# A one-layer hybrid recurrent step: the RWKV head norm reordered, delta-net inputs loaded at another place, state waits narrowed

## The reference, cut to what matters

```python
# end of RWKV (C), per head of 64 columns
mu  = mean(o_c);  var = mean(square(o_c - mu))
o_c = (o_c - mu) * rsqrt(var + GN_EPS) * ln_w + ln_b
bonus = sum(r_c * k_c * r_k) * v_c
y_c = (o_c + bonus) * g_c                      # g_c = sigmoid(g_low) @ rwkv_g_up
# start of gated DeltaNet (A): causal convolution of width 4, then SiLU
full = concatenate([conv_buf, qkv]);  new_conv = full[:, t:]
# A and B: the samples start from a given state and return the new one
# merge of the three branches
m = sum_i sigmoid(P_gate_i) * (y_i @ w_branch[i]);  h = h + m @ w_out
```

## Time and profile before

| | us |
|---|---|
| median of three runs (lowest, highest) | 3218.73 (3212.09, 3221.67) |
| the profiled execution's own time | 3215.23 |
| span of the profiled execution | 3213.4 |
| PE busy in the span | 3080.0 |
| DVE, ACT, POOL busy | 1671.0, 1182.4, 109.9 |

### The profile page before, as it was taken

The page is one execution under the profiler, slowest core; times in us unless marked ns, Lnnn a source line. Parts: engine busy times, 40 slices in busy tenths (PEclk is TensorE's granted clock), DMA queues, the critical chain, the costliest instruction groups (busy, mean ns, idle before and its releaser), DMA issues.

```text
span 3213.4 us, 61472 instructions
## 1 busy us (share of the span) xinstructions
PE 3080.0 (96%) x24976; PEld 2966.6 (92%) x24976; DVE 1671.0 (52%) x2174; ACT 1182.4 (37%) x1589; POOL 109.9 (3%) x176
## 2 busy tenths in 40 slices
PE   8999999999899999999889998997999999999998
PEld 7999999999899888888888988886999999999998
DVE  5455445454545665555575546456455444445543
ACT  4343333333434532222253224344343333333333
POOL 1000000001000000000000001011000000000001
PEclk9999999999999999998989989989999999999999
DMA  5555555655455533334553336357545655555553
GB/s 166 166 157 169 172 157 164 171 161 171 124 170 149 152 109 95 90 105 117 166 148 95 101 115 184 108 175 252 165 131 161 170 165 170 158 169 157 167 170 112
DMA packets 599915, 482.51 MB, mean 150 GB/s; under 512 B 29010, under 2 KB 545597, under 8 KB 599389
## 3 DMA queue, kind: packets, MB, share of 16 engines
q1 hardware_dynamic: 575760, 428.45, 45.7%
q0 software_dynamic: 8592, 33.16, 3.4%
q10 hardware_dynamic: 15392, 18.43, 1.6%
HBM read 451.82 MB, written 28.10 MB: 149 GB/s over the span
## 4 chain that ended last, share of the span: by engine, by line
PE 85%; DVE 7%; ACT 3%; issue 2%; DMA 2%; ACTq 0%; POOL 0%; DVEq 0%; POOLq 0%
PE ps L392 25%; PE ps L393 24%; PE ps L394 24%; PE ps L1111 2%; DVE lo L749 2%; ACT hi L559 1%; PE ps L1106 1%; PE ps L1392 0%; DMA smA<-in_dt_bias 0%; PE ps L551 0%; PE ps L2308 0%; PE ps L1405 0%; DMA rawsD<-kept 0%; PE ps L1935 0%; DVE raws L773 0%
## 5 line engine op out<-in xcount | busy, mean ns | idle before, releaser
L392 PE MATMUL ps<-xh,hi 128*128 128x288 f32 x4800 | 1456.4, 303 | 45.7 <-ACT kept L630 11.2
L393 PE MATMUL ps<-xl,hi 128*128 128x288 f32 x4800 | 1430.0, 298 | 0.0
L394 PE MATMUL ps<-xh,lo 128*128 128x288 f32 x4800 | 1429.1, 298 | 0.0
L749 DVE TENSOR_TENSOR lo<-raw,hi 128x1024 fp32r<-128x1024 f32 (+1 forms) x820 | 975.1, 1213 | 542.8 <-ACT hi L559 533.2
L559 ACT ACTIVATE hi<-raw 128x1024 fp32r<-128x1024 f32 (+1 forms) x820 | 832.5, 1042 | 843.3 <-PE ps L394 797.6
L392 PEld LDWEIGHTS ps<-xh,hi 128*128 128x128 f32 x4800 | 915.9, 191 | 77.8 <-issue 25.1
L393 PEld LDWEIGHTS ps<-xl,hi 128*128 128x128 f32 x4800 | 916.2, 191 | 0.6
L394 PEld LDWEIGHTS ps<-xh,lo 128*128 128x128 f32 x4800 | 915.8, 191 | 0.0
L393 PE MATMUL ps<-hidl,hi 128*128 128x288 f32 x1376 | 406.9, 296 | 0.0
L392 PE MATMUL ps<-hidh,hi 128*128 128x288 f32 x1376 | 406.9, 296 | 0.0
L394 PE MATMUL ps<-hidh,lo 128*128 128x288 f32 x1376 | 404.3, 294 | 0.0
(11 more groups left out here) (680 smaller groups left out, 2022.0 us busy)
## 6 DMA issues: line engine op xcount, KB each, us to landing
raw<-in_w_ff_up SPq DMA_DIRECT2D x688, 256.0 KB, 4.1
raw<-in_w_in SPq DMA_DIRECT2D x448, 256.0 KB, 3.0
raw<-in_w_ff_down SPq DMA_DIRECT2D x344, 256.0 KB, 3.4
raw<-in_w_out SPq DMA_DIRECT2D x64, 256.0 KB, 3.0
raw<-in_w_branch SPq DMA_DIRECT2D x48, 256.0 KB, 3.0
gatesD<-kept ACTq DMA_DIRECT2D x24, 288.0 KB, 3.0
gates<-gatesD POOLq DMA_DIRECT2D x8, 864.0 KB, 7.2
raw<-in_w_branch SPq DMA_DIRECT2D x48, 128.0 KB, 3.4
```

The lines of the kernel that those rows point to most:

```text
L392: pe.matmul(out, w, rh, start=start, stop=False)
L393: pe.matmul(out, w, rl, start=False, stop=False)
L394: return pe.matmul(out, wl, rh, start=False, stop=stop)
L749: dve.tensor_tensor(lo[:, q, 0:wide], raw[:, q, 0:wide], hi[:, q, 0:wide].bitcast(F32), SUB).then_inc(lo_ready[q], 1)
```

## The change

The tail of RWKV takes another order: the product r·k·r_k is made before the mean, in a tile of its own (`rsF`); its head sum and the multiplication by v go ahead of the root; weight with bonus, and bias with gate, become one operation each, on six slices. PE no longer waits for `C_recurred`. The unit counts there become 2, 5, 2, 3 and 8. POOL loads `rowsA` and `smA` when RWKV's tail begins, A's projections when its last sum is made, and the first two sample states of A at `mixer_done`. The 36 tile copies of the delta-net head become two; the copy of the last rows moves behind the second turn of the loop, and an empty SiLU stands ahead of the loop. The wait for the prompt's state in A moves down to the first write that needs it, and in B it goes; B's first sample state is loaded without it. The units behind each pair of sample states in B rise from 4 to 8 (`bsso`). In `branch` ACT makes the merged high part after the next split; `out` loses its wait at the start. The waits on `sums_read` and `hn_sum` are counted anew.

```diff
@@ pe_program, phase
-                if not (down or name.startswith("up") and name != "up00" and name != "up10"):
+                if not (down or name == "out" or name.startswith("up") and name != "up00" and name != "up10"):
                     pe.wait_ge(acc_empty, p["group0"])
@@ act_program
+            def merged_high(k):
+                act.wait_ge(sem("gated"), k + 1)
+                pair = slice(2 * k, 2 * k + 2)
+                act.activation(xh[:, pair, :], merged[:, pair, :], ACT.Copy).then_inc(sem("merged_hi"), 1)
...
                             split(ahead(p, s, it))
                         if name == "branch":
+                            if s % 2 == 0 and it * 4 + s // 2:
+                                merged_high(it * 4 + s // 2 - 1)
...
-                        if name == "branch":
-                            act.wait_ge(sem("gated"), it * 4 + (g + 1))
-                            pair = bass.ds((it * 4 + g) * 2, 2)
-                            act.activation(xh[:, pair, :], merged[:, pair, :], ACT.Copy).then_inc(sem("merged_hi"), 1)
+                        if name == "branch" and it * 4 + g == KD // 2 - 1:
+                            merged_high(it * 4 + g)
@@ U
-  rec=6, fin=4, fin2=15, bsso=4
+  rec=2, fin=5, fin2=2, fin3=3, fin4=8, bsso=8
@@ pe_mixC
             weave(U["rec"])
-            e.need("C_recurred")
...
             weave(U["fin"])
-            e.need("hn_sq")
+            e.need("hn_sq", 2)
...
             weave(U["fin2"])
-            e.need("hn_sq")
+            e.need("sums_read", 2)
             for p in range(BT):
-                mm = pe.matmul(ps[:, p, 0:NT], ones64[:, :], sqF[:, p, :], start=True, stop=True)
+                mm = pe.matmul(ps[:, p, 0:NT], ones64[:, :], rsF[:, p, :], start=True, stop=True)
...
@@ dve_mixC
+            for p in range(BT):
+                ins = dve.scalar_tensor_tensor(rsF[:, p, :], proj[:, p, 0:NT], par1[:, R_RK + p:R_RK + p + 1], proj[:, 6 + p, 0:NT], MUL, MUL)
...
+            weave(U["rec"])
+            e.need("hn_sum", 2)
+            e.link(dve.scalar_tensor_tensor(Y, PS6, -1.0 / 64, Y, MUL, ADD))
+            e.mark(dve.tensor_tensor(sqF[:, :, :], Y, Y, MUL), "hn_sq")
+            dve.wait_ge(sem("C_so8_stored"), 6)
+            dve.nop().then_inc(sem("C_recurred"), 1)
             weave(U["fin"])
+            weave.presplit(2)
             e.need("hn_sum", 2)
-            e.mark(dve.tensor_tensor(sqF[:, :, :], PS6, proj[:, 12:18, 0:NT], MUL), "gn_bonus_used")
-            e.link(dve.tensor_tensor(Y, Y, sqF[:, :, :], ADD))
+            e.mark(dve.tensor_tensor(rsF[:, :, :], PS6, proj[:, 12:18, 0:NT], MUL), "gn_bonus_used")
+            weave(U["fin2"])
+            e.need("fin_rs")
+            e.link(dve.tensor_tensor(Y, Y, sqF[:, :, :], MUL))
+            for p in range(BT):
+                e.link(dve.scalar_tensor_tensor(Y[:, p, :], Y[:, p, :], par1[:, R_LNW + p:R_LNW + p + 1], rsF[:, p, :], MUL, ADD))
+            weave(U["fin3"])
             e.need("hn_sum")
-            e.link(dve.tensor_tensor(Y, PS6, Y, MUL))
+            for p in range(BT):
+                e.link(dve.scalar_tensor_tensor(Y[:, p, :], Y[:, p, :], par1[:, R_LNB + p:R_LNB + p + 1], ps[:, p, 0:NT], ADD, MUL))
+            weave(U["fin4"])
             dve.nop().then_inc(sem("mixer_done"), 1)
@@ pool_A
-            pool.wait_ge(sem("mixer_done"), 1)
             pool.dma_start(rowsA[0:24, :], ...).then_inc(sem("a_landed"), 16)
+            for k, name in ((0, "a_log"), (1, "dt_bias")):
+                pool.dma_start(smA[:, k, :], i[name][0].partition_broadcast(P)).then_inc(sem("a_landed"), 16)
             pool.wait_ge(sem("kept_stored"), 16 * GROUPS_A)
+            e.need("hn_sum", 5)
             for k in range(4):
                 pool.dma_start(proj[:, 6 * k:6 * k + 6, :], projA[:, 6 * k:6 * k + 6, :]).then_inc(sem("projA_landed"), 16)
...
+            pool.wait_ge(sem("mixer_done"), 1)
+            load_state(pool, tA[1], 0, "A", state_in, 3)
+            load_state(pool, tA[1], 1, "A", state_in, 3)
             e.need("rows_kept")
@@ pe_mixA
             pe.wait_ge(sem("a_landed"), 48)
+            pe.wait_ge(sem("mixer_done"), 1)
@@ act_mixA
             e.link(act.activation(smA[:, 0, :], smA[:, 0, :], ACT.Exp))
-            e.need("last_turned")
-            e.mark(act.activation(rowsA[0:27, :], psf[0:27, 512:512 + 2304], ACT.Copy), "rows_kept")
+            e.link(act.activation(spare, ones[:, 0:1], ACT.Silu))
+            e.need("last_kept", 2)
...
+                if m == 1:
+                    e.need("last_turned")
+                    e.mark(act.activation(rowsA[0:27, :], psf[0:27, 512:512 + 2304], ACT.Copy), "rows_kept")
                 weave(U["conv"])
@@ dve_mixA: two copies for 36; b == 2
+            e.link(dve.tensor_copy(tails[:, :, :, 0:GAP], ps[:, 0, 0:432].rearrange("p (m b t) -> p m b t", b=NSEQ, t=GAP)))
+            e.mark(dve.tensor_copy(lastA[:, :, GAP:27].rearrange("p m (b t) -> p m b t", t=GAP), tails[:, :, :, TS:]), "last_kept")
...
                     dve.nop().then_inc(sem("state_whole"), 1)
-                    dve.wait_ge(sem("state_stored"), 1)
...
+                if b == 2:
+                    dve.wait_ge(sem("state_stored"), 1)
                 e.link(dve.tensor_tensor(t["kb"][0:n, :, :], region(2, n, P), bc(R("nb"), 2, P), MUL))
@@ pool_B
+            load_state(pool, tB[1], 0, "B", state_in, 2)
             pool.wait_ge(sem("out_stored"), 16 * stored)
-            pool.nop().then_inc(sem("state_stored"), 2)
+            load_state(pool, tB[1], 1, "B", state_in, 2)
@@ dve_mixB
             rest_y(dve, 0, BT)
+            weave.presplit(2)
             e.need("B_gl")
...
                     dve.nop().then_inc(sem("state_whole"), 1)
-                    dve.wait_ge(sem("state_stored"), 2)
```

More of the change, by code:

```diff
@@ L1212, in dve_solve @@
             weave(next(units))
-        U = dict(feat=6, hist=12, shift=60, rec=6, root=3, bfeat=8, lora=6, lora2=3, kk=8, prod=7, tok=2,
-                 wz=2, z=1, scz=1, sco=2, s0t=2, ssz=2, szt=2, sso=3, s8t=2, fin=4,
+        U = dict(feat=6, hist=12, shift=60, rec=2, root=3, bfeat=8, lora=6, lora2=3, kk=8, prod=7, tok=2,
+                 wz=2, z=1, scz=1, sco=2, s0t=2, ssz=2, szt=2, sso=3, s8t=2, fin=5,
                  conv=3, head=8, hl=8, aba=4, gc=6, aprod=7, az=4, ascz=2, asco=6, assz=2, asso=3,
-                 bgk=20, fin2=15, hn=8, afin=6, afin2=8, bfin=2, bfin2=16, bprod=4, bsco=6, bsso=4)
+                 bgk=20, fin2=2, fin3=3, fin4=8, hn=8, afin=6, afin2=8, bfin=2, bfin2=16, bprod=4, bsco=6, bsso=8)
         def pool_mixers(pool):
@@ L1519, in act_mixC @@
             act_root_of(e, act, sqF, 1.0 / 64, 1, 2, weave)
-            weave(U["fin2"] - U["root"] + 2 * U["fin"])
+            weave(U["fin2"] + U["fin3"] + U["fin4"] - U["root"])
         def act_root_of(e, act, sq_, scale, k, sums, weave):
@@ L1734, in dve_mixC @@
                     e.mark(ins, "hn_sq")
+            weave(U["rec"])
[4 more added lines that the diff above has]
+            dve.nop().then_inc(sem("C_recurred"), 1)
             weave(U["fin"])
+            weave.presplit(2)
             e.need("hn_sum", 2)
-            e.mark(dve.tensor_tensor(sqF[:, :, :], PS6, proj[:, 12:18, 0:NT], MUL), "gn_bonus_used")
-            e.link(dve.tensor_tensor(Y, Y, sqF[:, :, :], ADD))
-            weave(U["fin"])
+            e.mark(dve.tensor_tensor(rsF[:, :, :], PS6, proj[:, 12:18, 0:NT], MUL), "gn_bonus_used")
[4 more added lines that the diff above has]
+                e.link(dve.scalar_tensor_tensor(Y[:, p, :], Y[:, p, :], par1[:, R_LNW + p:R_LNW + p + 1], rsF[:, p, :], MUL, ADD))
+            weave(U["fin3"])
             e.need("hn_sum")
-            e.link(dve.tensor_tensor(Y, PS6, Y, MUL))
+            for p in range(BT):
+                e.link(dve.scalar_tensor_tensor(Y[:, p, :], Y[:, p, :], par1[:, R_LNB + p:R_LNB + p + 1], ps[:, p, 0:NT], ADD, MUL))
+            weave(U["fin4"])
             dve.nop().then_inc(sem("mixer_done"), 1)
@@ L1799, in pool_A @@
             pool.dma_start(gkupB[:, :], i["gla_gk_up"][0]).then_inc(sem("gk_landed"), 16)
-            for k, name in ((0, "a_log"), (1, "dt_bias")):
-                pool.dma_start(smA[:, k, :], i[name][0].partition_broadcast(P)).then_inc(sem("a_landed"), 16)
+            state_in = lambda h: i["state_gdn"][0, :, h].rearrange("b k v -> k b v")
+            pool.wait_ge(sem("mixer_done"), 1)
+            load_state(pool, tA[1], 0, "A", state_in, 3)
+            load_state(pool, tA[1], 1, "A", state_in, 3)
             e.need("rows_kept")
@@ L1812, in pool_A, with load_state @@
             pool.nop().then_inc(sem("state_stored"), 1)
-            return sample_states(pool, e, stored, tA[1], 6, "A",
-                                 lambda h: i["state_gdn"][0, :, h].rearrange("b k v -> k b v"),
+            pool.wait_ge(sem("A_decays_spent"), 1)
+            load_state(pool, tA[1], 2, "A", state_in, 3)
```

(29 more changed lines are left out.)

15 lines of the change are left out of this document (removed).

## The result

Five runs of the changed kernel have a median of 3186.81 us (3184.97 to 3191.72); five of the kernel before have 3221.67. The ratio is 0.9892, with a 95% interval of 0.9873 to 0.9912: 35 us faster (28 to 41). The forecast was 3172, the range 3156 to 3195. The main case's own range, 3163 to 3181, was missed by 6 us. The first three runs of before that the forecast started from had a median of 3218.73, and the execution whose profile it was worked from took 3215.23; later medians of before lie at 3219 to 3223, so 6 us of the difference are in the starting point.

The account below looks back on a forecast made before the run. PE, busy in 96% of the span, was taken to bound the kernel. Eight terms sum to 44.1 us: 3171.1 from the profiled 3215.2, 3174.6 from the median; it said 3172, range 3156 to 3195.

Parts of the forecast that it names:

- main case: Whole kernel: the eight terms' gains come together, 3172 us, with its own range 3163 to 3181; chance 0.50.
- Term 1: RWKV tail and delta-net head up to the convolution: new order and earlier loads gain 16.0 us (12 to 18.4).
- Term 2: Convolution and norms: table load moves under the copies, last rows' copy sits in ACT's second turn; gain 1 (-2 to +3).
- Term 3: A's samples: DVE's wait for POOL's store moves below the decay chain; gain 6.8 us, 3.4 if the clock stays.
- Term 4: B's head: one more slot is split while DVE waits for its gates; gain 3 us (0 to 5.5).
- Term 5: B's samples, first block: DVE's 3.7 us wait for POOL goes, loads start earlier; gain 4 us (2 to 5.3).
- Term 7: Branch merge: split before high part saves DVE up to 10.6 us, transfers may limit; half taken, 5.5 (2 to 10.6).
- Term 8: Start of `out`: without the wait PE begins 1.9 us after the last branch product; gain 4.8 us (3 to 5.5).
- Term 6: B's sample states: twelve more branch units lift the clock; gain 3 us, -7 if it stays low, +9 if wholly lifted.
- waits handed on: Rival: PE's waits pass one for one to RWKV, convolution and merge; gain 8.4, 3207 to 3210 us, chance 0.06.
- transfers decide: Rival: merge bound by DMA gains nothing, projections hold weights back, PE stands about 5; 3182 to 3185 us, chance 0.21.
- The other rivals: Better, 3159 or 3160 us, chance 0.20; change not doing what it says, 3207 to 3210, 0.06; slower, 3229, 0.03.

Follow-up runs that it names:

- y4: Changed kernel with A's projections loaded after the end of RWKV, some 6 us later: 3188.66 us, ratio 0.9897 to the kernel before.
- x1: Kernel before with only the RWKV tail, the early loads and the delta-net head changed: 3202.51 us, ratio 0.9941.
- x3: Kernel before with only the two state waits at the third blocks of A and B narrowed: 3211.25 us, ratio 0.9972.
- z4: Changed kernel with an eighth of the gates loaded for the merge's last four pairs, so its output differs: 3183.66 us, ratio 0.9877 to the kernel before.
- x4: Kernel before with only eight units instead of four behind each pair of B's sample states: 3214.84 us, ratio 0.9979.
- y3: Changed kernel, eight units kept, DVE walking four ahead of its state update and four behind: 3176.44 us, ratio 0.9870 to the kernel before.
- y5: Changed kernel with five more units behind the gate sums in RWKV's tail (13 for 8): 3170.18 us, ratio 0.9839 to the kernel before.
- z3: Changed kernel with one more unit behind the gate sums in RWKV's tail (9 for 8): 3179.29 us, ratio 0.9866 to the kernel before.
- y2: Changed kernel with four units again behind each pair of B's sample states: 3180.51 us, ratio 0.9870 to the kernel before.

## Why the prediction came out as it did

The direction and the range were right, and eight tenths of the gain came. By its own steps:

- **Term 1** (16.0) measured 16.8. The order worked out was right in its one new wait (1.8 forecast, 1.4 in the trace) and in the projections landing in time: the last was there by 1591.8 (issued at 1579.9, at most 11.9 us to land), 3 us before DVE copied the tails beside them at 1595.0, and in y4, loaded later, PE stood. The copies cost 1.0 us instead of the 1.4 taken.
- **Term 2** (1): 0.6, but not by its steps. The table load did not move under the copies: DVE's copies ended at 1596.3, ACT loaded the table at 1602.91, behind splits and drains, and DVE waited 4.5 us for the first tap behind it. PE's waits for drains fell from 8.4 to 3.2 us, and one of 3.3 for a low part is new. That this comes out near 1 is luck.
- **Term 3** (6.8): 6.9 in the first pair of traces. **Term 4** (3): 1.6 in the first pair; over five traces with the old head (10.0 to 12.2 lost) and six with the new one and 13 units fewer (5.1 to 8.5) the means differ by 3.8; no run takes this part alone. **Term 5** (4): 3.9. Measured alone, terms 3 and 5 won 5 to 12 where 10.8 was forecast. They are not independent of the rest: in x1, where A's wait stood in its old place, PE lost 1.6 us in A's third block instead of 7.2, and 9.2 in B's instead of 5.7. That moving the wait is enough is shown by x3 (0.3 and 0.6 lost), that it is needed is not.
- **Term 7** (5.5): 5.2. Both limits that it weighed are there: in the first trace transfers stretch the third pair to 8.5 us, and DVE runs the others at 5.3 to 6.2. DMA's share was 0.95 over the whole merge, and z4 shows the part that transfers hold. But the half that the term took was a guess: over the nine traces the stage's loss fell by 1.6 to 6.0, so that 5.2 came so near is in part luck.
- **Term 8** was too small, 4.8 for 7.3: PE began 0.1 us behind the last branch product, not 1.9, because the low part of `out`'s first slot was made before that product ended, and the clock's 2.0 went whole.
- **Term 6** is the step that failed: +3 forecast, -4.8 measured. Its own mechanism is real: x4 won 2 to 12 us, and where PE hardly stands (0.5 us at most), the five traces with eight units lost 7.5 us to the low level in the mean (5.1 to 8.5), the five with four units 10.5 (8.5 to 12.9), which are the 3 us forecast. (The +9 for a wholly lifted clock isn't worked out in the prediction; the 12 us lost are what the clock could give there at most.) What failed is the premise ahead of the terms, that a unit used elsewhere costs the same and only their number counts. Thirteen units fewer in RWKV moved each later walk by one unit against the slots of four; in B's sample states the last unit of DVE's walk then met a low part behind a drain, with the state update queued behind it. There PE stood 5.9 us and lost 10.2 to the low level. Two edits of different kinds remove the standing: the order of walk and update (y3), and the offset (y5, z3). The prediction had named a longer stage there as a sign that term 6 is reversed, but waits handed on only for other places.

Between the gain forecast, 44, and that of the medians, 35, lie 9 us. In the pair of traces term 6 makes 7.8 of them, and taking the standing away won 7 us (y2) and 11 (y3) between medians; the other rows can't be added up against the medians, because the two rows of chance alone are 12 us. The result lies near the time of *transfers decide* (3182 to 3185), but not for its reason: PE did not stand 5 us at the projections, and the merge did give. The other rivals did not happen.

Left open is what the five units of y5 won beyond the standing, some 9 us between it and z3, whose intervals just overlap. Part of it is in B's head; it was not isolated.

## What to carry to other kernels

When several engines walk one list of work each at its own pace, count not only how many items stand at a place but where in a slot they begin: taking 13 out at one place changed what was met 500 us later. Let the engine that others wait for do the dependent step first and its share of the list behind it. And compare traces by what the bounding engine lost in each stage, not by lengths, and look at a stage whose code is the same in both before believing a difference of a few microseconds.

## What the hardware showed

The clock's low stretches differ between executions of the same instructions: up to RWKV's tail, where the code is the same in all 14 traces, PE lost between 18.9 and 31.8 us to the low level, and the runs of the kernel before ranged from 3212 to 3230.

In B's sample states the mean granted clock was 0.60 to 0.71 in the five traces with four units to a pair, and 0.77 to 0.84 in the nine with eight, whether PE stood there or not. A part of that rise says only that more wide products, many of them at the full level, lengthen the stage. The loss itself fell with more units where PE hardly stood, from 10.5 to 7.5 us in the mean, and not clearly where it stood (10.2 in all four traces). The Trainium skill (TensorE: Matmul & The Clock Gate, What's actually happening) states that activity releases the throttled state; these traces agree as far as the direction goes, and in none was the whole stage at the full level. But PE's being recorded busy didn't release it: in the kernel before PE was busy for all 32.30 us of the window in the earlier trace rows at a clock of 0.63, which bears the rule out less than the prediction said.
